# The last 32 tokens' expert rows by indirect DMA on VectorE, and the dense expert stage for 224 tokens

## The chip, the cores and the metric

One core of one Trainium2 chip runs the whole program. The metric is the device time of one execution in microseconds (us). The kernel before takes 1393.69 us, the median of 3 runs (1393.54 to 1394.06).

## The reference, cut to what matters

Two transformer blocks follow each other on 256 tokens of width 1024. The change touches only the last stage, the expert layer (PEER) of the second block. For each token, 8 heads choose 16 experts each out of 16384 (128 rows i by 128 columns j of a key grid), and each chosen expert e contributes gate * gelu(x . u_e) * v_e:

```python
def step(args):
    xc, ic, gc = args                 # tokens, chosen experts, gates
    u = expert_u[ic]
    hval = jnp.einsum('cd,chkd->chk', xc, u).astype(jnp.float32)
    a = (gc * jax.nn.gelu(hval, approximate=False)).astype(xc.dtype)
    return jnp.einsum('chk,chkd->cd', a, expert_v[ic])
```

The sum is added to the residual, and a last rms norm gives the output. All is float32.

## The kernel before, in words

The kernel gathers nothing. It computes the expert layer densely: U times x for all 16384 experts, the exact gelu, a dense matrix of gates that is zero for experts that were not chosen, the product of the two, and V times it. Experts go in 128 blocks of 128 (`NE`), in the order of the list `ORDER`.

Every weight of the program comes as a unit of 128 x 1024 float32 (512 KB). Four buffers each of `raw`, `wh` and `wl` hold it: SyncE issues the load, ScalarE rounds it to the high part (`high`, L1588, type fp32r), VectorE subtracts to get the low part (`low`, L567), and TensorE makes three fp32r products for each tile: high by high, high by low, low by high. So one unit costs ScalarE one pass of 1024 elements, VectorE one, and TensorE 6144 streamed columns. A buffer comes free when the step behind it is done, four units later. Each engine's order is the order of the code; there is no scheduler.

The expert layer has these stages.

- **U** (`early`, 128 units). The output is experts by tokens. Here the weights are the stationary operand and the 256 tokens are streamed. There are two forms. `unit_M` streams `hTb`, which holds the high and low parts of the tokens side by side, as 512 columns against the high weights, and 256 columns against the low weights: 16 matmuls. The second half of the bank must then be added to the first, by a copy on ScalarE (`block_out`) and a sum on VectorE (`summed`, or `both` early on). `unit_E` makes 24 matmuls of 256 columns, all into the same 256 columns, and needs neither. Units 0 to 31 and 48 to 127 take `unit_M`, units 32 to 47 `unit_E`. ScalarE then writes the gelu into `gates`.
- **Beside it**, during U units 0 to 47, VectorE does the two rounds of top-16 selection (`sixteen`, `at_rank` and what stands between, in slots of one `low` each). `best` tells that the choice is known.
- **G** (64 chunks of 4 tokens, one after each of U units 48 to 111). VectorE and ScalarE build one-hot rows (`oj`, `oi`), four plain float32 matmuls of 128 x 128 x 128 (eight instructions in the trace) multiply them out, and the chunk of gates is multiplied into what gelu has written, by `gated` and the lines behind it for what comes later.
- **V** (`unit_D`, 128 units). The output is tokens by 1024. Here the tokens' parts of `gates` are the stationary operand (two halves of 128 tokens, made by `high_of` and `low_of`), and the weights are streamed: 12 matmuls of 512 columns. The last four units are cut so that the tail can begin early.

GpSimd has nothing to do in all this. SyncE issues all DMAs. SBUF is filled to the end by `gates` (128 x 128 x 256 float32).

## Time and profile before

| | |
|---|---|
| median of 3 runs | 1393.69 us |
| span of the profiled execution | 1391.9 us |
| around the span (median less span) | 1.8 us |
| TensorE busy | 1379.2 us (99%) |
| VectorE busy | 1012.8 us (73%) |
| ScalarE busy | 850.9 us (61%) |
| GpSimd busy | 43.0 us (3%) |
| DMA, share of 16 engines in queue 1 | 53.1% |
| granted TensorE clock | 1.000 of 2.4 GHz |
| U stage begins, V stage begins | about 620 us, 1037 us |

A busy TensorE here means that a matmul is in flight; matmuls are pipelined and overlap, so the time of a piece of work is read from the distance between starts, not from the mean duration. The slices of the span show where an engine has room; the idle time in front of a group of instructions, and who ended it, tells what it waited for.

### The profile page before, as it was taken

Reading aid. Unit: us, or ns where it says so; the run is one execution under the profiler, and the core shown is the slowest. Engines: PE = TensorE matmul, PEld = TensorE weight load, DVE = VectorE, ACT = ScalarE, POOL = GpSimd, SP = SyncE. Lnnn points to the kernel's source line nnn. Section 1 sums busy time; section 2 is a strip of 40 time slices with the busy share of each in tenths; the row PEclk is TensorE's granted clock in tenths of the full one; section 3 lists DMA queues with packets and bytes.
Section 4 is the critical chain, followed back from the end, with each engine's and each line's share of the span. In section 5 each row is a group of like instructions: output and inputs, shape, how many; then the busy total and the mean of one; then the engine's idle time right before and its main releaser. Section 6 shows DMA issues by size and latency. Waiting matters only on the chain.

```text
span 1391.9 us, 20882 instructions
## 1 busy us (share of the span) xinstructions
PE 1379.2 (99%) x7704; PEld 1196.5 (86%) x7704; DVE 1012.8 (73%) x1926; ACT 850.9 (61%) x1647; POOL 43.0 (3%) x49
## 2 busy tenths in 40 slices
PE   8999999999999999999999999999999999999998
PEld 6998888888898888888899999999888888888886
DVE  6877776666786667689998888889776555555555
ACT  6875655555665554546767888888565455444554
POOL 3002030000000000000000000000000000000000
PEclk9999999999999999999999999999999999999999
DMA  6533466555444446545564444444466655566653
GB/s 228 183 113 129 143 216 190 188 182 182 165 158 146 137 152 226 188 161 165 184 202 158 142 151 137 149 139 144 160 213 222 214 193 192 192 195 195 194 191 101
DMA packets 67563, 240.85 MB, mean 173 GB/s; under 512 B 8453, under 2 KB 8965, under 8 KB 67078
## 3 DMA queue, kind: packets, MB, share of 16 engines
q1 hardware_dynamic: 67462, 239.52, 53.1%
q8 instruction: 62, 1.02, 0.3%
q14 instruction: 39, 0.32, 0.1%
HBM read 237.39 MB, written 2.10 MB: 172 GB/s over the span
## 4 chain that ended last, share of the span: by engine, by line
PE 94%; DVE 3%; ACT 2%; issue 1%; DMA 0%; POOL 0%; SPq 0%; POOLq 0%; ACTq 0%; DVEq 0%
PE bank L2239 92%; PE bank L2337 1%; PE bank L2325 1%; DVE wl L567 1%; ACT wh L1588 0%; DMA x<-in_x 0%; ACT kdz L1594 0%; DVE St L757 0%; DVE x L1066 0%; DVE sgt L1064 0%; DVE t L717 0%; DVE sg L711 0%; POOL st L487 0%; ACT h L1604 0%; DVE St L754 0%
## 5 line engine op out<-in xcount | busy, mean ns | idle before, releaser
L567 DVE TENSOR_TENSOR wl<-raw,wh 128x1024 fp32r<-128x1024 f32 x429 | 522.8, 1225 | 230.0 <-ACT wh L1588 229.0
L1588 ACT ACTIVATE wh<-raw 128x1024 fp32r<-128x1024 f32 x429 | 449.1, 1055 | 230.2 <-PE bank L2239 226.8
L2239 PE MATMUL bank<-hTb,wh 128*128 128x512 f32 (+2 forms) x1952 | 587.4, 363 | 0.0
L2239 PE MATMUL bank<-hTb,wl 128*128 128x256 f32 (+1 forms) x1640 | 432.7, 280 | 0.0
L2239 PE MATMUL bank<-wh,hTb 128*128 128x512 f32 (+1 forms) x1496 | 427.1, 392 | 0.9 <-DVE hTb L601 0.8
L2239 PEld LDWEIGHTS bank<-hTb,wh 128*128 128x128 f32 (+1 forms) x1952 | 341.2, 188 | 46.1 <-issue 0.3
L2239 PEld LDWEIGHTS bank<-wh,hTb 128*128 128x128 f32 x1496 | 281.1, 189 | 59.3 <-DVE wl L567 1.0
L2239 PEld LDWEIGHTS bank<-hTb,wl 128*128 128x128 f32 (+1 forms) x1640 | 309.5, 189 | 11.6
L2239 PE MATMUL bank<-wl,hTb 128*128 128x512 f32 (+1 forms) x748 | 245.9, 389 | 0.0
L2239 PEld LDWEIGHTS bank<-wl,hTb 128*128 128x128 f32 x748 | 141.2, 189 | 28.2
L2239 PEld LDWEIGHTS bank<-oi,oj 128*128 128x128 f32 x512 | 67.0, 191 | 2.9
L2239 PE MATMUL bank<-oi,oj 128*128 128x128 f32 x512 | 67.4, 274 | 0.0
L1594 ACT ACTIVATE us<-bank 128x256 f32<-128x256 f32 x80 | 30.2, 377 | 57.4 <-PE bank L2239 57.4
L1514 DVE TENSOR_TENSOR hTb<-gates,hTb 128x256 fp32r<-128x256 f32 x126 | 52.6, 418 | 0.0
L487 POOL TENSOR_TENSOR st<-st,mhalf 128x1 f32<-128x1 f32 (+2 forms) x15 | 13.1, 875 | 1269.9 <-DVE st L581 1000.2
L1594 ACT ACTIVATE hTb<-gates 128x256 fp32r<-128x256 f32 x126 | 50.3, 400 | 0.0
L1493 DVE TENSOR_TENSOR us<-bank,us 128x256 f32<-128x256 f32 x80 | 33.2, 415 | 17.4 <-ACT us L1594 17.4
L1475 DVE TENSOR_TENSOR oj<-iota,jT 128x512 f32<-128x512 f32 x64 | 43.6, 682 | 1.9 <-ACT gT L1594 1.9
L1487 DVE TENSOR_TENSOR gates<-gates,ga 128x256 f32<-128x256 f32 (+32 forms) x79 | 24.8, 314 | 25.2 <-ACT gates L2119 24.3
L2175 ACT ACTIVATE oi<-iota,iT 128x128 f32<-128x128 f32 x128 | 40.6, 391 | 0.0
L2179 ACT ACTIVATE oi<-oi,gT 128x128 f32<-128x128 f32 x128 | 40.6, 389 | 0.0
L1479 DVE TENSOR_SCALAR oi<-iota,iT,gT 128x128 f32<-128x128 f32 x128 | 35.5, 340 | 0.0
(396 smaller groups left out, 1264.2 us busy)
## 6 DMA issues: line engine op xcount, KB each, us to landing
raw<-in_wts SPq DMA_DIRECT2D x441, 512.0 KB, 4.2
x<-in_x SPq DMA_DIRECT2D x4, 256.0 KB, 5.2
sk<-in_sk SPq DMA_DIRECT2D x1, 1024.0 KB, 7.8
spill<-x SPq DMA_DIRECT2D x1, 1024.0 KB, 7.3
x<-spill SPq DMA_DIRECT2D x1, 1024.0 KB, 6.3
gb<-in_g_ffn SPq DMA_DIRECT2D x1, 512.0 KB, 4.8
gb<-in_norm_mix_g SPq DMA_DIRECT2D x1, 512.0 KB
gb<-in_norm_ffn_g SPq DMA_DIRECT2D x1, 512.0 KB, 5.7
```

What stands on the lines that cost most here:

```text
L567: e.tensor_tensor(b[:, :], raw[u % RAW][:, :], a[:, :].bitcast(F), ALU.subtract).then_inc(S("lo"), 1)
L1475: e.tensor_tensor(oj[c % NB][:, :, :], big, bc(jT[:, t], 2, 128), ALU.is_equal).then_inc(S("oj"), 1)
L1479: e.tensor_scalar(oi[c % NB][:, k, :], iota[:, :], iT[:, a], gT[:, a], ALU.is_equal, ALU.mult).then_inc(S("oi"), 1)
L1487: e.tensor_tensor(g[:, 0:c], g[:, 0:c], ga[n % 4][:, 0:c], ALU.mult).then_inc(S("gated_2"), 1)
L1493: e.tensor_tensor(u, B[2 + n % 4][:, 0:256], u, ALU.add).then_inc(S("u_sum"), 1)
L1514: e.tensor_tensor(b, gates[:, ORDER[n], :], a.bitcast(F), ALU.subtract).then_inc(S("al"), 1)
L1588: e.activation(parts_of(u)[0][:, :], raw[u % RAW][:, :], ACT.Copy).then_inc(S("hi"), 1)
L1594: return e.activation(o, i, ACT.Copy)
L2175: i = own.up(e.activation(oi[m][:, k, :], iota[:, :], ACT.Abs, scale=-1.0, bias=iT[:, t:t + 1]))
L2179: e.activation(oi[m][:, k, :], oi[m][:, k, :], ACT.Relu, scale=-2.0, bias=gT[:, t:t + 1]).then_inc(S("oi_act"), 1)
L2239: return e.matmul(o, l, r, start=first, stop=last, skip_group_check=True)
L2325: p = e.transpose(B[turned_at(t, i)[0]][:, two(128, k)], src[:, q, 512 * j + 128 * k:512 * j + 128 * k + 128], ident[:, :])
```

## The change

The expert layer is split by tokens. Tokens 0 to 223 (`TN`) stay in the dense form, with 224 in the place of 256 in U, gelu, gates and V, and 56 chunks of G (`NC`) for 64. Tokens 224 to 255 (partitions 96 to 127 of the second half) leave it: GpSimd copies their normalised rows, their experts' numbers and their gates to the layout 32 tokens by 4 groups of 32 choices, and then issues 64 indirect DMAs of 128 rows x 4 KB each, 32 from `u_rows` and 32 from `v_rows` (the same numbers in their plain layout in HBM), into three buffers. VectorE makes a dot product out of each of the first 32 (a fused multiply and sum), ScalarE one gelu, and VectorE multiplies each of the last 32 by its factor and adds it up. Three small DMAs bring the four groups together and VectorE adds them to the residual. These 64 slots stand in VectorE's order behind every second U unit from unit 104 (11 slots), and behind every second V unit (53 slots, up to V unit 106).

Besides, U units 0 to 31 and 48 to 103 change from `unit_M` to `unit_E`, all units below 104 being now 24 matmuls of 224 columns; units 104 to 127 (`SUMMED` on) stay `unit_M`, with 448 and 224 columns. In V the second half has 96 tokens; the streamed columns remain 512. The buffers for this come out of the smaller `gates`. Some semaphores are merged and their counts shifted.

```diff
 NP, NB = 47, 5
+TN = 224
+NC = TN // 4
+SUMMED = NP + 1 + NC
+SLOTS = 32
...
-        gates = M("gates", [128, 128, 256])
-        ga = [M(f"ga{i}", [128, 256]) for i in range(4)]
-        us = [sb("us0", [128, 256], F, X0 + 5120), M("us1", [128, 256])]
+        gates = M("gates", [128, 128, TN])
+        ga = [M(f"ga{i}", [128, TN]) for i in range(4)]
+        us = [sb("us0", [128, TN], F, X0 + 5120), M("us1", [128, TN])]
+        xr = sb("xr", [128, 1024], F, M.p)
+        acc = M("acc", [128, 1024])
+        ROWS = M.p
+        rows = [M(f"rows{i}", [128, 1024]) for i in range(3)]
+        fold = sb("fold", [128, 3, 1024], F, ROWS)
+        tq = sb("tq", [128, 2, 512], F, ROWS)
+        picked = sb("picked", [128, 128], U32, ROWS + 8192)
+        weight = sb("weight", [128, 128], F, ROWS + 8704)
+        expert = M("expert", [128, SLOTS], U32)
+        gate_of = M("gate_of", [128, SLOTS])
+        dots = M("dots", [128, SLOTS])
+        factor = M("factor", [128, SLOTS])
...
+        def used_by(j):
+            return j + 1 + 2 * (j >= SLOTS)
+        def slots_taken():
+            at = [n for n in range(SUMMED, NE - 2, 2)]
+            left = 2 * SLOTS - len(at)
+            return at, {2 * k + (2 if len(at) + k >= SLOTS else 0): len(at) + k for k in range(left)}
...
+            def four_ways(dst, src):
+                for a in range(4):
+                    e.dma_start(dst(a), src(a)).then_inc(S("in_few"), 16)
+            e.wait_ge(S("h"), 16)
+            four_ways(lambda a: xr[32 * a:32 * a + 32, :], lambda a: h5[96:128, 1, :])
+            e.wait_ge(S("in_few"), 64)
+            e.wait_ge(S("best"), 7)
+            four_ways(lambda a: expert[32 * a:32 * a + 32, :], lambda a: picked[96:128, two(SLOTS, a)])
+            four_ways(lambda a: gate_of[32 * a:32 * a + 32, :], lambda a: weight[96:128, two(SLOTS, a)])
+            e.wait_ge(S("in_few"), 192)
+            for j in range(2 * SLOTS):
+                if j >= 3:
+                    e.wait_ge(S("used"), used_by(j - 3))
+                k = j % SLOTS
+                e.indirect_dma_start(
+                    out=rows[j % 3][:, :], out_offset=None, in_=I["u_rows"] if j < SLOTS else I["v_rows"],
+                    in_offset=bass.IndirectOffsetOnAxis(ap=expert[:, k:k + 1], axis=0)).then_inc(S(f"in_rows{j % 3}"), 16)
+            e.wait_ge(S("used"), used_by(2 * SLOTS - 1))
+            for a in range(3):
+                e.dma_start(fold[96:128, a, :], acc[32 * a:32 * a + 32, :]).then_inc(S("in_few"), 16)
...
-                elif n < 16 + EARLY:
-                    n -= 16
-                    v = lows_of[:, n % 2, :]
-                    e.wait_ge(S("u_out"), nth_sum("U", n))
-                    e.tensor_tensor(v, B[2 + n % 4][:, 0:256], v, ALU.add).then_inc(S("u_sum"), 1)
...
+            few = slice(96, 128)
+            e.wait_ge(S("best"), 5)
+            e.wait_ge(own.sem, own.n)
+            e.scalar_tensor_tensor(out=picked[few, :].rearrange("p (h k) -> p h k", h=8), in0=ij[few, 0, 1, :, :],
+                                   scalar=128.0, in1=ij[few, 1, 1, :, :], op0=ALU.mult, op1=ALU.add).then_inc(S("best"), 1)
+            e.tensor_copy(weight[few, :].rearrange("p (h k) -> p h k", h=8), bst[few, 1, :, :]).then_inc(S("best"), 1)
...
+            def slot_taken(j):
+                t, k = rows[j % 3], j % SLOTS
+                e.wait_ge(S(f"in_rows{j % 3}"), 16 * (j // 3 + 1))
+                if j == 0:
+                    e.wait_ge(S("in_few"), 192)
+                if j < SLOTS:
+                    e.tensor_tensor_reduce(out=t[:, :], in0=t[:, :], in1=xr[:, :], scale=1.0, scalar=0.0, op0=ALU.mult,
+                                           op1=ALU.add, accum_out=dots[:, k:k + 1]).then_inc(S("used"), 1)
+                    return
+                if j == SLOTS:
+                    e.wait_ge(S("used"), used_by(SLOTS - 1) + 1)
+                    e.tensor_tensor(factor[:, :], factor[:, :], gate_of[:, :], ALU.mult).then_inc(S("used"), 1)
+                    e.wait_ge(S("used"), used_by(SLOTS - 1) + 2)
+                    e.tensor_scalar(acc[:, :], t[:, :], factor[:, 0:1], None, ALU.mult).then_inc(S("used"), 1)
+                    return
+                e.wait_ge(S("used"), used_by(j - 1))
+                e.scalar_tensor_tensor(out=acc[:, :], in0=t[:, :], scalar=factor[:, k:k + 1], in1=acc[:, :], op0=ALU.mult,
+                                       op1=ALU.add).then_inc(S("used"), 1)
+            def folded(a):
+                xs = x[few, 1, :]
+                if a == 0:
+                    e.wait_ge(S("in_end"), 48)
+                    e.wait_ge(S("used"), used_by(2 * SLOTS - 1))
+                    e.tensor_tensor(xs, xs, acc[few, :], ALU.add).then_inc(S("used"), 1)
+                    e.wait_ge(S("in_few"), 240)
+                e.wait_ge(S("used"), used_by(2 * SLOTS + a))
+                e.tensor_tensor(xs, xs, fold[few, a, :], ALU.add).then_inc(S("used"), 1)
...
-            for c in range(64):
+            for c in range(NC):
                 n = NP + 1 + c
-                summed(n)
                 low(nth("U", ORDER[n]) + 2)
-                if c + NB - 1 < 64:
+                if c + NB - 1 < NC:
                     one_hots(c + NB - 1)
                 gated(n)
...
+            at_u, at_v = slots_taken()
+            for n in range(SUMMED, NE - 2):
                 summed(n)
                 low(nth("U", ORDER[n]) + 2)
                 gated(n)
                 if n in (NE - 6, NE - 5):
                     low_of(n - NE + 6)
+                if n in at_u:
+                    slot_taken(at_u.index(n))
...
+                if n in at_v:
+                    slot_taken(at_v[n])
+                elif n - 6 in (max(at_v), max(at_v) + 1, max(at_v) + 2):
+                    folded(n - 6 - max(at_v))
...
-                if EARLY <= n <= NP:
+                if n < SUMMED:
                     e.wait_ge(S("done"), nth("U", ORDER[n]) + 1)
                 else:
                     e.wait_ge(S("u_sum"), nth_sum("U", n))
-                    b = lows_of[:, n % 2, :] if n < EARLY else us[n % 2]
+                    b = us[n % 2]
                 if c:
                     if n >= NP + 6:
                         e.wait_ge(S("gated_2"), n - NP - 5)
                     t = e.activation(ga[n % 4][:, 0:c], b[:, 0:c], ACT.Gelu)
-                if c < 256:
-                    t = e.activation(gates[:, ORDER[n], c:256], b[:, c:256], ACT.Gelu)
+                if c < TN:
+                    t = e.activation(gates[:, ORDER[n], c:TN], b[:, c:TN], ACT.Gelu)
                 t.then_inc(S("gelu"), 1)
             def block_out(n):
                 e.wait_ge(S("done"), nth("U", ORDER[n]) + 1)
-                if n < 2:
-                    e.wait_ge(S("u_sum"), nth_sum("w_peer_q_2", 14 + n))
-                elif n < EARLY:
-                    e.wait_ge(S("gelu"), n - 1)
-                copy(lows_of[:, n % 2, :] if n < EARLY else us[n % 2][:, :],
-                     B[2 + n % 4][:, 256:512]).then_inc(S("u_out"), 1)
+                copy(us[n % 2][:, :], B[2 + n % 4][:, TN:2 * TN]).then_inc(S("u_out"), 1)
...
-            for n in range(EARLY):
-                block_out(n)
-                if n:
-                    gelu(n - 1)
-                else:
-                    scores_out(3)
+            high(nth("U", ORDER[0]) + LOOK)
+            scores_out(3)
+            for n in range(39):
+                gelu(n)
...
+                if n == after_dots:
+                    e.wait_ge(S("used"), used_by(SLOTS - 1))
+                    e.activation(factor[:, :], dots[:, :], ACT.Gelu).then_inc(S("used"), 1)
...
-            def unit_E(unit, o, turned=None):
+            def unit_E(unit, o, turned=None, width=256):
                 wh_, wl_ = begin(unit)
                 for k in range(8):
                     c = two(128, k)
                     if turned is not None and k in (0, 4):
                         e.wait_ge(S("hT_lo"), 4 * turned + 3 + k // 4)
-                    mm(o, wh_[:, c], hTh[:, k, :], k == 0, False)
-                    mm(o, wh_[:, c], hTl[:, k, :], False, False)
-                    t = mm(o, wl_[:, c], hTh[:, k, :], False, k == 7)
+                    mm(o, wh_[:, c], hTh[:, k, 0:width], k == 0, False)
+                    mm(o, wh_[:, c], hTl[:, k, 0:width], False, False)
+                    t = mm(o, wl_[:, c], hTh[:, k, 0:width], False, k == 7)
...
-                        mm(bank[:, 0:256], wl_[:, c], hTh[:, k, :], False, False)
-                    t = mm(bank[:, :], wh_[:, c], hTb[:, :, k, :], k == 0, k == 7)
+                        mm(bank[:, 0:width], wl_[:, c], hTh[:, k, 0:width], False, False)
...
-            def part_D(held, xh, xl, base, q, first, last):
-                s = two(128, q)
+            def part_D(held, xh, xl, base, q, first, last, tokens=128):
+                s = slice(128 * q, 128 * q + tokens)
                 for a, b, f, z in ((xh, held[0], first, False), (xh, held[1], False, False), (xl, held[0], False, last)):
                     for n in range(2):
-                        t = mm(B[base + 2 * q + n][:, :], a[:, s], b[:, two(512, n)], f, z)
+                        t = mm(B[base + 2 * q + n][0:tokens, :], a[:, s], b[:, two(512, n)], f, z)
...
-                if n < EARLY or n > NP:
-                    unit_M(("U", ORDER[n]), B[2 + n % 4])
+                if n >= SUMMED:
+                    unit_M(("U", ORDER[n]), B[2 + n % 4], width=TN)
                 else:
-                    unit_E(("U", ORDER[n]), B[2 + n % 4][:, 0:256])
+                    unit_E(("U", ORDER[n]), B[2 + n % 4][:, 0:TN], width=TN)
...
-                unit_D(("D", "peer_expert_v_2", ORDER[n]), *of_expert(n), 0, n == 0, False)
+                unit_D(("D", "peer_expert_v_2", ORDER[n]), *of_expert(n), 0, n == 0, False,
+                       tokens=(rows_of(0), rows_of(1)))
...
-                        t = mm(end_of(c), a[:, 128:256], b[:, c], f, False)
+                        t = mm(end_of(c)[0:rows_of(1), :], a[:, 128:TN], b[:, c], f, False)```

TensorE in the stage with the gates: one U unit and the one-hot products behind it. Names are `hTb` for the tokens, `wh` and `wl` for high and low weights; the last number is the streamed width. Before:

```order
L2239 MATMUL bank<-oi_201,oj_196 128x128 x4
L2239 MATMUL bank<-hTb,wh_57 128x512
L2239 MATMUL bank<-hTb,wl_61 128x256
L2239 MATMUL bank<-hTb,wh_57 128x512
L2239 MATMUL bank<-hTb,wl_61 128x256
L2239 MATMUL bank<-hTb,wh_57 128x512
```

and the same place of the kernel after:

```order
L2332 MATMUL bank<-oi_201,oj_196 128x128 x4
L2332 MATMUL bank<-hTb,wh_57 128x224 x2
L2332 MATMUL bank<-hTb,wl_61 128x224
L2332 MATMUL bank<-hTb,wh_57 128x224 x2
L2332 MATMUL bank<-hTb,wl_61 128x224
L2332 MATMUL bank<-hTb,wh_57 128x224 x2
```

A pair of 512 and 256 columns has become a triple of 224 columns, eight times in a unit.

VectorE behind the last gate chunks, where U units go on without them (`us` is the sum of a bank's halves, `wl` the low part of a unit, `rows` and `dots` belong to the new slots). Before:

```order
L1493 TENSOR_TENSOR us_211<-bank,us_211 128x256
L567 TENSOR_TENSOR wl_62<-raw_54,wh_58 128x1024
L1487 TENSOR_TENSOR gates<-gates,ga_207 128x256
L1493 TENSOR_TENSOR us_212<-bank,us_212 128x256
L567 TENSOR_TENSOR wl_59<-raw_51,wh_55 128x1024
L1487 TENSOR_TENSOR gates<-gates,ga_208 128x256
```

and after:

```order
L1552 TENSOR_TENSOR us_211<-bank,us_211 128x224
L623 TENSOR_TENSOR wl_62<-raw_54,wh_58 128x1024
L1546 TENSOR_TENSOR gates<-gates,ga_207 128x224
L1561 ISA rows_215,dots<-rows_215,xr 128x1024
L1561 ISA dots 128x1
L1552 TENSOR_TENSOR us_212<-bank,us_212 128x224
L623 TENSOR_TENSOR wl_59<-raw_51,wh_55 128x1024
```

The dot product stands between one unit's product with the gates and the next unit's sum, and so ahead of the next unit's low part.

VectorE in the V stage, after (before, the rows L1561 are not there):

```order
L623 TENSOR_TENSOR wl_59<-raw_51,wh_55 128x1024
L1603 TENSOR_TENSOR hTb<-gates,hTb 128x224
L1561 ISA rows_217,dots<-rows_217,xr 128x1024
L1561 ISA dots 128x1
L623 TENSOR_TENSOR wl_60<-raw_52,wh_56 128x1024
L1603 TENSOR_TENSOR hTb<-gates,hTb 128x224
L623 TENSOR_TENSOR wl_61<-raw_53,wh_57 128x1024
```

One slot stands behind two units' low parts.

## Rows read from the trace of the kernel before

**Rows 1.** The page's busy line: busy us (share of the span) xinstructions.
```profile
PE 1379.2 (99%) x7704; PEld 1196.5 (86%) x7704; DVE 1012.8 (73%) x1926; ACT 850.9 (61%) x1647; POOL 43.0 (3%) x49
```

**Rows 2.** The chain of waits, end of it: start us, us, engine and line.
```profile
670.67 82.92 PE bank L2239 x584
754.25 620.40 PE bank L2239 x3304
1377.43 3.05 PE bank L2239 x12
```

**Rows 3.** Busy us (xinstructions) of each engine by stretch; clock, DMA share, GB/s.
```profile
660.00:711.00 51.00, 50.96 (x292) 44.23 (x291) 49.98 (x142) 34.74 (x58) 0.00 (x0) 1.00 0.56 186
711.00:757.00 46.00, 46.00 (x386) 46.00 (x386) 43.39 (x123) 31.54 (x52) 0.00 (x0) 1.00 0.62 205
800.00:900.00 100.00, 100.00 (x656) 90.70 (x656) 86.70 (x192) 84.33 (x247) 0.00 (x0) 1.00 0.46 143
992.00:1037.00 45.00, 45.00 (x259) 39.18 (x258) 32.34 (x51) 26.77 (x50) 0.00 (x0) 1.00 0.56 180
1087.00:1380.00 293.00, 292.92 (x1292) 242.28 (x1292) 167.32 (x215) 145.78 (x215) 0.00 (x0) 1.00 0.58 187
```

**Rows 4.** Timeline of TensorE, unit_M without gates: start us, us, instruction xcount.
```profile
1002.86 0.40 PE L2239 MATMUL bank<-hTb,wl 128*128 128x256 f32 x2
...
1011.31 0.40 PE L2239 MATMUL bank<-hTb,wl 128*128 128x256 f32 x2
1011.55 0.63 PE L2239 MATMUL bank<-hTb,wh 128*128 128x512 f32 x2
```

**Rows 5.** Timeline of TensorE, unit_E.
```profile
728.95 0.40 PE L2239 MATMUL bank<-hTb,wh 128*128 128x256 f32 x2
...
729.31 0.40 PE L2239 MATMUL bank<-hTb,wh 128*128 128x256 f32 x2
```

**Rows 6.** Timeline of TensorE, a gate chunk and a U unit in turn.
```profile
770.80 1.05 PE L2239 MATMUL bank<-oi,oj 128*128 128x128 f32 x8
771.61 0.48 PE L2239 MATMUL bank<-hTb,wh 128*128 128x512 f32 x1
...
774.47 1.05 PE L2239 MATMUL bank<-oi,oj 128*128 128x128 f32 x8
```

**Rows 7.** Timeline of TensorE, plain float32 products of 64 columns.
```profile
427.48 1.00 PE L2239 MATMUL bank<-v2b,PT 128*128 128x64 f32 x8
```

**Rows 8.** Timeline of TensorE, plain float32 products of 256 columns.
```profile
77.10 0.59 PE L2239 MATMUL bank<-kTn,qTn 128*128 128x256 f32 x2
77.53 0.59 PE L2239 MATMUL bank<-kTr,qTr 128*128 128x256 f32 x2
```

**Rows 9.** Timeline of TensorE, V stage; then a unit with 64 stationary columns.
```profile
1141.00 0.62 PE L2239 MATMUL bank<-wl,hTb 128*128 128x512 f32 x2
...
1142.36 0.62 PE L2239 MATMUL bank<-wl,hTb 128*128 128x512 f32 x2
...
25.16 0.39 PE L2239 MATMUL bank<-hTb,wh 128*64 128x256 f32 x2
...
25.50 0.39 PE L2239 MATMUL bank<-hTb,wh 128*64 128x256 f32 x2
```

**Rows 10.** VectorE, U units without gates: start us, us, instruction [idle before, releaser].
```profile
1009.59 0.42 DVE L1493 TENSOR_TENSOR us<-bank,us 128x256 f32<-128x256 f32 x1 [0.93 <-ACT us L1594]
1009.93 1.21 DVE L567 TENSOR_TENSOR wl<-raw,wh 128x1024 fp32r<-128x1024 f32 x1
```

**Rows 11.** VectorE groups by form: busy us, mean ns | idle us before, releaser.
```profile
L561 DVE SCALAR_TENSOR_TENSOR wl<-raw,gpc,wh 128x1024 fp32r<-128x1024 f32 x8 | 10.1, 1280 | 3.1 <-ACT wh L1585 3.1
...
L567 DVE TENSOR_TENSOR wl<-raw,wh 128x1024 fp32r<-128x1024 f32 x107 | 131.2, 1226 | 124.1 <-ACT wh L1588 124.1
```

**Rows 12.** DMA issues: KB each, median us to landing.
```profile
raw<-in_wts SPq DMA_DIRECT2D x103, 512.0 KB, 4.3
```

More of the change, by code:

```diff
@@ L1514, in low_of @@
                 e.tensor_tensor(b, gates[:, ORDER[n], :], a.bitcast(F), ALU.subtract).then_inc(S("al"), 1)
-            for n in range(NP + 65, NE - 2):
+            at_u, at_v = slots_taken()
+            for n in range(SUMMED, NE - 2):
                 summed(n)
@@ L1537, in add_end @@
                     c, b = two(512, 1), B[3][:, :]
-                e.tensor_tensor(x[:, 1, c], b, x[:, 1, c], ALU.add).then_inc(S("x"), 1)
+                xs = x[0:rows_of(1), 1, c]
+                e.tensor_tensor(xs, b[0:rows_of(1), :], xs, ALU.add).then_inc(S("x"), 1)
             def weighted_end(n):
                 c = ENDS[n]
+                e.wait_ge(S("used"), used_by(2 * SLOTS + 3))
                 e.wait_ge(S("x"), 19 + n)
@@ L2140, in keys_out @@
                 copy(key[a][:, s, :, :], bc(f4[:, s, a, :], 3, 16)).then_inc(S("key"), 1)
-            for n in range(EARLY):
-                block_out(n)
-                if n:
-                    gelu(n - 1)
-                else:
-                    scores_out(3)
+            high(nth("U", ORDER[0]) + LOOK)
+            scores_out(3)
+            for n in range(39):
+                gelu(n)
                 if n in (18, 19, 21, 23):
                     keys_out(0, n // 20, n % 18 in (1, 5))
-            high(nth("U", ORDER[EARLY]) + LOOK)
-            for n in range(EARLY - 1, 39):
-                gelu(n)
-                if 33 <= n < 37:
+                elif 33 <= n < 37:
                     keys_out(1, (n - 33) // 2, (n - 33) % 2)
@@ L2184, in scalar @@
             gelu(NP)
-            for c in range(64):
+            for c in range(NC):
                 n = NP + 1 + c
-                block_out(n)
-                if c + NB - 1 < 64:
+                if c + NB - 1 < NC:
                     one_hots(c + NB - 1)
@@ L2204, in high_of @@
                 copy(of_expert(n)[0], gates[:, ORDER[n], :]).then_inc(S("ah"), 1)
-            for n in range(NP + 65, NE - 2):
+            for n in range(SUMMED, NE - 2):
                 block_out(n)
@@ L2256, in unit_E, with unit_M @@
                         e.wait_ge(S("hT_lo"), 4 * turned + 3 + k // 4)
-                    mm(o, wh_[:, c], hTh[:, k, :], k == 0, False)
-                    mm(o, wh_[:, c], hTl[:, k, :], False, False)
-                    t = mm(o, wl_[:, c], hTh[:, k, :], False, k == 7)
+                    mm(o, wh_[:, c], hTh[:, k, 0:width], k == 0, False)
+                    mm(o, wh_[:, c], hTl[:, k, 0:width], False, False)
+                    t = mm(o, wl_[:, c], hTh[:, k, 0:width], False, k == 7)
                 t.then_inc(S("done"), 1)
-            def unit_M(unit, bank, turned=None):
+            def unit_M(unit, bank, turned=None, width=256):
                 wh_, wl_ = begin(unit)
@@ L2303, in unit_K, with unit_D @@
                 t.then_inc(S("done"), 1)
-            def part_D(held, xh, xl, base, q, first, last):
-                s = two(128, q)
+            def part_D(held, xh, xl, base, q, first, last, tokens=128):
+                s = slice(128 * q, 128 * q + tokens)
                 for a, b, f, z in ((xh, held[0], first, False), (xh, held[1], False, False), (xl, held[0], False, last)):
                     for n in range(2):
-                        t = mm(B[base + 2 * q + n][:, :], a[:, s], b[:, two(512, n)], f, z)
+                        t = mm(B[base + 2 * q + n][0:tokens, :], a[:, s], b[:, two(512, n)], f, z)
                 return t
-            def unit_D(unit, xh, xl, base, first, last, half=False):
+            def unit_D(unit, xh, xl, base, first, last, half=False, tokens=(128, 128)):
                 held = begin(unit)
                 for q in range(2):
-                    t = part_D(held, xh, xl, base, q, first, last)
+                    t = part_D(held, xh, xl, base, q, first, last, tokens[q])
                     if q == 0 and half:
@@ L2971, in tensor @@
             early(NP)
-            for c in range(64):
+            for c in range(NC):
                 early(NP + 1 + c)
@@ L2986, in tensor @@
                 p.then_inc(S("G_ps"), 1)
-            for n in range(NP + 65, NE):
+            for n in range(SUMMED, NE):
                 early(n)
```

66 lines of the change are left out of this document (37 added, 29 removed).

## The prediction

> **What bounds the kernel now.** I read the busy line first: TensorE is busy for 1379.2 of 1391.9 us, VectorE for 73%, ScalarE for 61% [rows 1]. The chain of waits agrees: its last links are TensorE alone, one of them 620.40 us long without a break, from 754.25 to 1374.65 [rows 2]. Next come the busy times by stretch. TensorE fills every stretch of the expert layer, its clock is the higher level throughout (1.00, so 2.4 GHz), and VectorE comes near to it in one place only, beside the first U units: 49.98 of 51 us and 43.39 of 46 us [rows 3]. So only a shorter TensorE stream can shorten the program, as long as VectorE, which now gets 64 large operations more, and the DMA engines still feed it in time. Since matmuls overlap, I price them by the distance between starts.
>
> **Prices on TensorE, from the rows.** A `unit_M` takes (1011.31 - 1002.86)/3 = 2.817 us, or 0.352 for a pair of 512 and 256 columns [rows 4]. A triple of 256 columns takes 729.31 - 728.95 = 0.36, so 0.120 each and 2.88 for a `unit_E` [rows 5]. A gate chunk and its U unit take 774.47 - 770.80 = 3.67, so the chunk costs 0.85 [rows 6]. In V six matmuls of 512 columns take 1.36, 0.2267 each and 2.72 a unit [rows 9]. From 256 to 512 columns the pitch grows by 0.1067, which is 0.417 ns a column, one column at each tick of 2.4 GHz; on top of the columns there are 13 ns.
>
> By columns alone, 224 would take 0.120 - 32 x 0.417 ns = 0.1067. But there is a floor under a narrow matmul: eight plain ones of 128 columns last 1.05, and eight of 64 columns last 1.00 [rows 6, 7]. Half the columns save 7 ns each and not 27 or more. Less the 0.28 that one of them lasts, the pitch is 0.77/7 = 0.110 for 128 and 0.103 for 64 columns. I take the load of 128 stationary columns to be what is left, and it is no smaller for fp32r of 224 columns. So I use 0.110 for 224 columns; the ends are 0.1067 (columns alone) and 0.120 (the narrower matmul brings nothing, since no row has an fp32r matmul below 256 columns).
>
> The Trainium skill, "TensorE: Matmul & The Clock Gate", section "Back-to-back issue gap", gives N/2.4 + 2.5 ns for the isolated warm matmul. That is 96 ns for 224 columns, and by it the time would be some 35 us below my forecast. The trace disagrees with it for this type: 256 columns take 120 ns [rows 5] where the rule has 109. The same page, section "LDWEIGHTS (loading the stationary operand)", has columns/1.2, so 107 ns for 128 of them, which would be the floor; as an estimate by this page the time would be about 8 us below mine. The sum below uses neither.
>
> **The change, part by part.**
>
> U stage, before: 112 `unit_M` x 2.817 = 315.5, 16 `unit_E` x 2.88 = 46.1, 64 chunks x 0.85 = 54.4; together 416.0. After: 104 `unit_E` of 224 columns at 24 x 0.110 = 2.64 make 274.6. 24 `unit_M` have pairs of 448 and 224 columns: 0.352 less 27 ns for the 64 columns less 7 to 10 ns for the other, 0.318, so 2.54 each and 61.1. 56 chunks make 47.6. Together 383.3: **32.7 us less**. With 0.1067 it is 42, with 0.120 only 6. The number of matmuls rises (24 for 16 in 88 units), which is why narrower streams do not bring the full eighth: in those units the change of form alone would cost 0.06 each.
>
> V stage: the 12 matmuls stream the weights, 512 columns each, for 96 tokens as for 128. Nothing goes by columns. The load of the stationary operand is shorter: with 64 stationary columns a triple of 256 takes 25.50 - 25.16 = 0.34 instead of 0.36 [rows 5, 9], 6.7 ns a matmul. Half of that for 96 columns, on 6 matmuls in 124 units, is **2.5 us less** (bounds 0 and 5).
>
> VectorE and ScalarE beside U units 0 to 103: the sums (0.42) and ScalarE's copies go. In the busiest stretch, where VectorE has 49.98 of 51 us [rows 3] at 2.82 a unit, it needs 0.42 less while TensorE needs 0.18 less, so it falls behind nowhere. In units 32 to 47, where no sum goes, its 43.39 us less one or two sums are at most 2.7 a unit against 2.64. That is even, and the lead of up to three units that it enters with covers the difference (bounds 0 and 1). With the gates it was busy for 86.7% [rows 3], 3.18 of 3.67; then 2.8 of 3.49. Cost 0. The two small operations that pack experts and gates are beside units that TensorE still has before it. Cost 0.
>
> The slots in the U stage: 11 of them. VectorE's own work is at hand: behind each TensorE unit it waits 0.93 for ScalarE's copy, then sum, then low part, which ends at 1009.93 + 1.21 = 1011.14, while TensorE needs it at 1011.55 + 0.23 = 1011.78 [rows 4, 10]. The lead is only 0.64, because `low` looks two units ahead here. The period shrinks by 0.28, narrower operations give back 0.05: lead 0.41, idle time 0.70. A fused multiply and sum is not in the trace; the nearest row is the 128x1024 operation with a scalar and two tensors, 1280 ns [rows 11], and I add 0.1 for the small instruction that follows it. 1.38 against 0.70 pushes the next sum, the low part behind it and the TensorE unit that waits for it: 0.68 - 0.41 = 0.27 each, **3 us more** for 11. If the fused one makes two passes (2.5), it is 1.4 each, 15 us; below, nothing.
>
> The slots in the V stage: 53, each behind two units. VectorE idles (1.226 busy, 124.1/107 = 1.16 idle before each low part [rows 11]) for 2.3 in two units, so 1.28 fits, and even 2.5 nearly does. `low` runs three units ahead here and waits for the release of a buffer, so nothing on TensorE waits. ScalarE's one gelu and the last additions fit into its 50% of idle time. Cost 0, and 4 at worst.
>
> The row transfers: 64 x 512 KB more. In V the DMA engines are at 0.58 for 187 GB/s [rows 3]. 53 transfers in 53 x 5.44 us are 96 GB/s on top, 283 in all, share 0.88 if it grows in step. A weight load lands in 4.3 us [rows 12]. It is issued when a low part ends, about 2.4 us behind the release of its buffer, and needed four units (10.9) behind that release, so it may take about 8.5. A row transfer is issued three slots ahead, 16 us. I take cost 0. No row shows an indirect transfer or any issued by GpSimd; the lower end is the weight load's 4.3, the upper one is open and is a rival below. The Trainium skill, "DMA: Bandwidth & Descriptors", section "Anatomy of one DMA — SWDGE (gpsimd) path", has 2.0 us + bytes/436 GB/s for GpSimd's DMAs, an estimate of 3.2 us here; no run here shows it.
>
> SyncE's queue keeps its order; GpSimd's one is empty at that time, and its last norm comes after the last row transfer, long before it is asked for.
>
> **Sum.** -32.7 - 2.5 + 3.0 = -32.2. The profiled span 1391.9 becomes 1359.7; the 1.8 us between span and median stay: **1361.5 us**.
>
> **Rivals.**
>
> (B) The narrow matmul brings nothing. fp32r at 224 columns keeps 0.117 to 0.120. For it: 13 ns stand on top of the columns at 256, and no row shows what they become below 256. Against: with 64 stationary columns 256 takes 0.113, so the stream itself is not the floor. The gain from U is 6 to 14, the time about 1385.
>
> (C) The slots can't be fed: row transfers or the fused operation are slow, VectorE stands in a slot, and the low parts behind it are late. For it: 32 more MB, a path unseen in the trace, one in-order VectorE that also feeds TensorE. Against: three buffers and 16 us. It decides from the point where a transfer takes more than one slot's 5.44 us in steady state; the gain is used up at 5.44 + 32.2/53 = 6.05. At 7 us it is 83 us more, about 1444; with a two-pass fused operation alone about 1374.
>
> (D) fp32r loses its single pass below some width, and all 224 columns streams with it. Plain float32 takes (77.53 - 77.10)/2 = 0.216 for 256 columns [rows 8], two ticks a column, where fp32r takes one. For it: every fp32r matmul of the trace streams at least 256 columns, so a limit there would never have shown. Against: nothing in the rows speaks for a limit. 224 columns would take 0.189, `unit_E` 4.54: 104 x 1.90 + 24 x 8 x 0.079 = 213 more, **1574 us**. If each plain float32 product's both instructions came back, some 2070. It decides from a pitch of 0.110 + 32.2/2496 = 0.123.
>
> **How the numbers follow.** Forecast 0.60, with its own range 1346 (columns alone, slots free, V's 5) to 1377 (two-pass dot). B 0.13, C 0.13, D 0.12, and 0.02 for what I do not see, a pitch of 0.096 (about 1326) among it. 8 times in 10 the time lies between 1346 and 1396: forecast, B and the mild part of C; D and the rest of C are left out. Within 0.2% (2.8 us, about what a measurement of this kernel can tell from no change) is 0.03, out of B and C. Faster has the forecast, most of B and a third of C, 0.76; slower 0.21.
>
> **What would show it.** In the profile after: a triple of 224 columns at 0.33 (0.32 columns alone, 0.36 is B, 0.57 or more is D); the U stage 383 us long; V units at 2.70 and no idle time of TensorE in V; waits of TensorE for the low part of 0.3 us at every second unit from 104 on; the fused operation at about 1.3. Rows L1561 with idle time ended by a DMA are C. I am wrong if the pitch of 224 columns leaves 0.107 to 0.120, or if TensorE waits in V at all.

## The result and the profile after

The kernel after takes **1372.34 us** (median of 4 runs, 1371.71 to 1373.34), the kernel before beside it 1393.62 (1393.48 to 1394.06): ratio **0.9847, interval 0.9833 to 0.9861**, faster by 21.3 us. The forecast was 1361.5 with a range of 1346 to 1396. The direction was right and the time lies in the range, but a third of the forecast gain is missing: 21.3 instead of 32.1 us.

The page's busy line after, which answers to [rows 1], with its DMA lines for GpSimd's queue and for the weights. PE is TensorE, PEld its weight loads, DVE VectorE, ACT ScalarE, POOL GpSimd.

```profile
PE 1357.3 (99%) x8344; PEld 1184.8 (86%) x8344; DVE 1045.3 (76%) x1909; ACT 804.7 (59%) x1512; POOL 159.7 (12%) x128
...
q0 software_dynamic: 9808, 34.51, 6.5%
...
raw<-in_wts SPq DMA_DIRECT2D x441, 512.0 KB, 3.5
```

TensorE remains the bound at 99%. The chain of waits shows where it is broken (start us, us, engine and line), against [rows 2]:

```profile
581.19 164.12 PE bank L2332 x1368
745.96 256.53 PE bank L2332 x2152
1002.56 350.11 PE bank L2332 x1536
```

The one link of 620 us has become two, and the gap between the last two rows, at 1002.5, is less than 0.1 us: 745.96 + 256.53 = 1002.49. So TensorE still works almost without a pause, and what is missing must be in how long its instructions take. The busy times by stretch, against [rows 3] (behind the comma PE, PEld, DVE, ACT, POOL, each with its instructions; then the clock, the DMA share and GB/s):

```profile
660.00:711.00 51.00, 51.00 (x459) 51.00 (x459) 47.78 (x141) 28.67 (x43) 0.00 (x0) 1.00 0.64 205
800.00:900.00 100.00, 100.00 (x898) 100.00 (x897) 81.48 (x169) 77.39 (x225) 0.00 (x0) 1.00 0.45 148
948.00:1010.00 62.00, 61.93 (x391) 57.84 (x390) 55.64 (x95) 38.09 (x73) 20.74 (x11) 1.00 0.76 280
1087.00:1350.00 263.00, 263.00 (x1145) 199.41 (x1144) 196.47 (x243) 127.47 (x192) 64.64 (x40) 1.00 0.76 264
```

Two readings. In the first two rows the weight loads (second column of busy times) now fill the stretch just as the matmuls do: 51.00 of 51 and 100.00 of 100, where before they had 44.23 and 90.70. That alone does not show that the loads set the pace: the `unit_E` with 256 columns of before had 46.00 of 46 too [rows 3], at a pitch of 0.120; e5 and e6 below test it. In the last row TensorE has no idle time, but runs 1145 matmuls; the kernel before, in a stretch of the same length inside its V stage, runs 1162:

```profile
1087.00:1350.00 263.00, 263.00 (x1162) 217.82 (x1162) 151.20 (x194) 131.81 (x194) 0.00 (x0) 1.00 0.60 194
```

That is 229.7 against 226.3 ns a matmul. TensorE's clock is the higher level (1.00) in all five rows.

By stages, from first matmul to first matmul:

| stretch | before | after | change | forecast |
|---|---|---|---|---|
| up to the first U unit | 618.0 | 617.4 | -0.6 | 0 |
| U stage with gates | 419.1 | 392.8 | -26.4 | -29.7 |
| V stage, 124 units | 337.3 | 342.3 | **+5.0** | **-2.5** |
| the rest | 17.5 | 17.5 | 0.0 | 0 |

### The profile page after: what moved, and what is told of

It is laid out like the page before. It is cut to its first block, busy times and chain, and to the rows that moved or that the text cites. A ratio compares the mean times of both kernels' runs of the same rounds, so it can differ in the third digit from the quotient of the medians.

```text
span 1370.0 us, 22081 instructions
## 1 busy us (share of the span) xinstructions
PE 1357.3 (99%) x8344; PEld 1184.8 (86%) x8344; DVE 1045.3 (76%) x1909; ACT 804.7 (59%) x1512; POOL 159.7 (12%) x128
## 3 DMA queue, kind: packets, MB, share of 16 engines
q0 software_dynamic: 9808, 34.51, 6.5%
## 4 chain that ended last, share of the span: by engine, by line
PE 93%; DVE 3%; ACT 2%; issue 1%; DMA 0%; POOL 0%; POOLq 0%; SPq 0%; ACTq 0%; DVEq 0%
PE bank L2332 91%; PE bank L2430 1%; DVE wl L623 1%; PE bank L2418 1%; ACT wh L1686 0%; ACT kdz L1692 0%; DVE St L813 0%; DMA x<-in_x 0%; DVE h L648 0%; DVE x L1122 0%; POOL st L519 0%; ACT h L1702 0%; DVE sgt L1120 0%; DVE t L773 0%; DVE sg L767 0%
## 5 line engine op out<-in xcount | busy, mean ns | idle before, releaser
L623 DVE TENSOR_TENSOR wl<-raw,wh 128x1024 fp32r<-128x1024 f32 x429 | 523.2, 1226 | 177.7 <-ACT wh L1686 174.4
L2332 PE MATMUL bank<-hTb,wh 128*128 128x224 f32 (+4 forms) x2656 | 566.4, 305 | 0.1
L2332 PEld LDWEIGHTS bank<-hTb,wh 128*128 128x128 f32 (+1 forms) x2656 | 424.1, 191 | 19.9 <-issue 1.3
L2332 PE MATMUL bank<-hTb,wl 128*128 128x224 f32 (+2 forms) x1640 | 439.7, 276 | 0.0
L2332 PE MATMUL bank<-wh,hTb 128*128 128x512 f32 (+1 forms) x1496 | 429.7, 394 | 1.3 <-DVE hTb L657 1.0
L2332 PEld LDWEIGHTS bank<-wh,hTb 128*128 128x128 f32 (+1 forms) x1496 | 267.1, 179 | 76.7 <-DVE wl L623 1.7
L2332 PEld LDWEIGHTS bank<-hTb,wl 128*128 128x128 f32 (+1 forms) x1640 | 312.5, 191 | 5.1
L2332 PE MATMUL bank<-wl,hTb 128*128 128x512 f32 (+1 forms) x748 | 247.0, 391 | 0.0
L2332 PEld LDWEIGHTS bank<-wl,hTb 128*128 128x128 f32 (+1 forms) x748 | 134.2, 179 | 36.2
L600 POOL DMA_INDIRECT rows<-in_u_rows,expert x32 | 54.4, 1699 | 306.5 <-DVE dots L1561 303.0
L600 POOL DMA_INDIRECT rows<-in_v_rows,expert x32 | 54.6, 1705 | 127.6 <-DVE acc L1571 107.3
L2332 PE MATMUL bank<-oi,oj 128*128 128x128 f32 x448 | 59.6, 276 | 0.0
L2332 PEld LDWEIGHTS bank<-oi,oj 128*128 128x128 f32 x448 | 54.5, 192 | 0.0
L1546 DVE TENSOR_TENSOR gates<-gates,ga 128x224 f32<-128x224 f32 (+28 forms) x79 | 24.2, 306 | 35.8 <-ACT gates L2217 34.9
L1603 DVE TENSOR_TENSOR hTb<-gates,hTb 128x224 fp32r<-128x224 f32 x126 | 48.4, 385 | 0.0
L1692 ACT ACTIVATE hTb<-gates 128x224 fp32r<-128x224 f32 x126 | 47.1, 375 | 0.0
L1571 DVE SCALAR_TENSOR_TENSOR acc<-rows,factor,acc 128x1024 f32<-128x1024 f32 x31 | 39.7, 1279 | 0.0
L1561 DVE CUSTOM_DVE_ANT_0 rows<-rows,xr 128x1024 f32<-128x1024 f32 x32 | 39.0, 1219 | 0.0
## 6 DMA issues: line engine op xcount, KB each, us to landing
raw<-in_wts SPq DMA_DIRECT2D x441, 512.0 KB, 3.5
gb<-in_g_ffn SPq DMA_DIRECT2D x1, 512.0 KB
gb<-in_norm_mix_g SPq DMA_DIRECT2D x1, 512.0 KB
gb<-in_norm_ffn_g SPq DMA_DIRECT2D x1, 512.0 KB, 4.5
```

The costliest lines, as they stand in the source:

```text
L600: e.indirect_dma_start(out=rows[j % 3][:, :], out_offset=None, in_=I["u_rows"] if j < SLOTS else I["v_rows"], in_offset=bass.IndirectOffse ...
L623: e.tensor_tensor(b[:, :], raw[u % RAW][:, :], a[:, :].bitcast(F), ALU.subtract).then_inc(S("lo"), 1)
L1546: e.tensor_tensor(g[:, 0:c], g[:, 0:c], ga[n % 4][:, 0:c], ALU.mult).then_inc(S("gated_2"), 1)
L1561: e.tensor_tensor_reduce(out=t[:, :], in0=t[:, :], in1=xr[:, :], scale=1.0, scalar=0.0, op0=ALU.mult, op1=ALU.add, accum_out=dots[:, k:k + ...
L1571: e.scalar_tensor_tensor(out=acc[:, :], in0=t[:, :], scalar=factor[:, k:k + 1], in1=acc[:, :], op0=ALU.mult, op1=ALU.add).then_inc(S("used ...
L1603: e.tensor_tensor(b, gates[:, ORDER[n], :], a.bitcast(F), ALU.subtract).then_inc(S("al"), 1)
```

## The experiments

e1 to e4 ran on one chip, where the kernel before had a median of 1393.54 (10 runs), e5 to e8 on another, where it had 1393.99 (9 runs). Two theories start from the table. **S**: a load of 96 stationary columns, which I had priced as a gain of 2.5 us, makes V slower. **P**: in U the load of 128 stationary columns sets the pitch of narrow matmuls, so a pair of 448 and 224 columns, of which only one is narrow, is cheaper than a triple of 224. The rivals of S are the row transfers and slots. Loading 96 columns and writing 96 rows of output are one and the same change here, so no run parts the two.

**e1, a whole stationary operand in V.** `whole(n)` is the full buffer in the place of its 224 columns.

```
-                unit_D(("D", "peer_expert_v_2", ORDER[n]), *of_expert(n), 0, n == 0, False,
-                       tokens=(rows_of(0), rows_of(1)))
+                unit_D(("D", "peer_expert_v_2", ORDER[n]), *(of_expert(n) if n < 2 else whole(n)), 0, n == 0, False,
+                       tokens=(128, 96 if n < 2 else 128))
...
```

> The kernel after, but V units 2 to 127 load 128 stationary columns in the second half again (columns 224 to 255 hold older values; the 32 rows that they make are never read). Theory S (the shorter load itself slows the 512-column matmuls: 2.76 us a V unit where it was 2.72): V units return to 2.72, 124 x 0.04 = 5 us faster than after, 1367. Rival T (traffic: row transfers and VectorE's slots read and write SBUF beside TensorE): V units stay at 2.76, 1372. My prediction's own term said that the shorter load gains 2.5 us; by it this kernel would be slower than after, 1375.

Measured: 1368.21 us (1367.1 to 1368.34), ratio 0.9815 (0.9802 to 0.9829), 4.1 below the kernel after. V takes 337.55 us. The timeline of TensorE in V, after and then e1 (start us, us, instruction):

```profile
1100.40 0.62 PE L2332 MATMUL bank<-wl,hTb 128*96 128x512 f32 x2
...
1101.78 0.63 PE L2332 MATMUL bank<-wl,hTb 128*128 128x512 f32 x2
...
1103.16 0.62 PE L2332 MATMUL bank<-wl,hTb 128*96 128x512 f32 x2
```

```profile
1199.81 0.62 PE L2332 MATMUL bank<-wl,hTb 128*128 128x512 f32 x2
...
1201.17 0.62 PE L2332 MATMUL bank<-wl,hTb 128*128 128x512 f32 x2
...
1202.53 0.62 PE L2332 MATMUL bank<-wl,hTb 128*128 128x512 f32 x2
```

Six matmuls take 1.38 us after and 1.36 in e1, the value of [rows 9]. Note that after, the halves with 128 and with 96 stationary columns both take 1.38: the slowdown is not confined to the matmuls that load 96. All slots and row transfers are still in e1, so they are not the cause. S holds.

**e2, no slots and no row transfers.**

```
-            for j in range(2 * SLOTS):
+            for j in range(0):
...
-                if n in at_u:
-                    slot_taken(at_u.index(n))
...
```

> The kernel after without the 64 indirect transfers, the 64 slots on VectorE, ScalarE's one gelu and the last additions (what the experts give to the last 32 tokens is left out). Theory S: V units stay at 2.76; only the waits of U units 104 to 127 go (61.7 us for 24 where 24 x 2.50 = 60.0), 1.7 us faster, about 1370.5. Rival T: V units return to 2.72 as well, 5 us more, about 1365.5. If the slots starved TensorE somewhere that I have not seen, more than that.

Measured: 1371.53 us (1370.78 to 1372.2), ratio 0.9841 (0.9826 to 0.9856), the same as the kernel after within what can be told. V's stretch in e2:

```profile
1087.00:1350.00 263.00, 263.00 (x1145) 199.44 (x1144) 145.85 (x192) 127.29 (x190) 0.00 (x0) 1.00 0.56 189
```

VectorE has 50 us less to do and the DMA engines 75 GB/s less to move, and TensorE still runs 1145 matmuls. In the U units from 104 on it is 1.3 us (60.40 for 61.67). So 64 large operations and 32 MB on a path that the trace of before did not have cost about one microsecond together in this kernel.

**e3, the kernel before with 96 columns in V's second half and nothing else.**

```
-                unit_D(("D", "peer_expert_v_2", ORDER[n]), *of_expert(n), 0, n == 0, False)
+                unit_D(("D", "peer_expert_v_2", ORDER[n]), *of_expert(n), 0, n == 0, False, tokens=(128, 96))
...
```

> The kernel before with 96 stationary columns in the second half of every V unit and nothing else of the change (32 tokens get nothing from the experts). Theory S: V units take 2.76 for 2.72, 5 us slower than before, 1398.7. Rival T: no difference, 1393.6. The prediction's term: 2.5 us faster, 1391.

Measured: 1398.82 us (1398.07 to 1399.39), ratio 1.0036 (1.0023 to 1.005): slower, by 5.3 us. TensorE's timeline in V:

```profile
1199.77 0.62 PE L2239 MATMUL bank<-wl,hTb 128*96 128x512 f32 x2
...
1201.15 0.63 PE L2239 MATMUL bank<-wl,hTb 128*128 128x512 f32 x2
...
1202.54 0.62 PE L2239 MATMUL bank<-wl,hTb 128*96 128x512 f32 x2
```

The same 1.385 as in the kernel after, out of a program that has only this part of the change. With e1 that is the effect from both sides: 4.1 us back when it is taken out, 5.3 us on top when it is put in (in V alone, by the traces, 4.8 and 5.0).

**e4, pairs beside the gates.** U units 48 to 103 go back to `unit_M` with 448 and 224 columns, with ScalarE's copy and VectorE's sum.

```
-SUMMED = NP + 1 + NC
+SUMMED = NP + 1
+TAIL = NP + 1 + NC
...
+                summed(n)
...
+                block_out(n)
...
```

> The kernel after with U units 48 to 103, those beside the gates, in pairs of 448 and 224 columns again, with ScalarE's copy and VectorE's sum. The trace after shows 0.3375 for a triple of 224 (2.70 a unit) and 0.312 for a pair of 448 and 224 (2.50 a unit). Theory P (TensorE sets the pace there, and the three products cost 0.2 a unit): 56 x 0.2 = 11 us faster than after, 1361. Rival Q (ScalarE, 3.08 us busy in a unit of the kernel before, or VectorE, 3.18, can't keep a pace of 3.37): waits of TensorE take half of it or more, 1367 to 1375.

Measured: 1363.93 us (1363.13 to 1365.03), ratio 0.9785 (0.9771 to 0.9798), 8.4 below the kernel after. The start of each gate chunk, after and then e4, and e4's busy times of that stretch:

```profile
751.15 1.06 PE L2332 MATMUL bank<-oi,oj 128*128 128x128 f32 x8
...
754.73 1.06 PE L2332 MATMUL bank<-oi,oj 128*128 128x128 f32 x8
```

```profile
802.03 1.05 PE L2335 MATMUL bank<-oi,oj 128*128 128x128 f32 x8
...
805.44 1.05 PE L2335 MATMUL bank<-oi,oj 128*128 128x128 f32 x8
```

```profile
800.00:900.00 100.00, 100.00 (x705) 96.50 (x705) 94.10 (x208) 88.23 (x263) 0.00 (x0) 1.00 0.47 156
```

The mean period of all chunks falls from 3.573 to 3.407, which is 9.3 us over 56. The expectation had 11 because it took 2.70 and 2.50 for units that take 2.68 and 2.52. VectorE rises from 81% to 94%. In the profiled run, the slowest of the five (1365.03), two pauses give part of it back: 1.8 us in the units from 104 on (63.51 for 61.67) and 0.8 in V (343.16 for 342.32). The first one (start us, us, instruction, idle time before it and what ended it):

```profile
990.21 1.06 ACT L1688 ACTIVATE wh<-raw 128x1024 fp32r<-128x1024 f32 x1 [1.91 <-DMA raw<-in_wts]
...
995.00 0.44 PE L2335 MATMUL bank<-hTb,wh 128*128 128x448 f32 x1 [1.89 <-DVE wl L624]
```

ScalarE waits for a weight load that lands late, the low part behind it is late too (a slot of VectorE stands between), and TensorE waits for it. In the kernel after ScalarE waits up to 2.16 us for a weight load at the start of V, and 2.08 at 1058, and TensorE never notices; without row transfers its longest such wait from 940 on is 1.41 (e2) and 1.81 (before), and both stand at the start of V. So P holds in its mechanism. That the row transfers make the loads late fits these rows, but was not tested in the kernel of e4.

**e5 and e6: what is the floor under a narrow matmul?** One run each. e5 streams 192 columns in the place of 224 in every `unit_E` of U, e6 loads 96 stationary columns in the place of 128.

```
-                    unit_E(("U", ORDER[n]), B[2 + n % 4][:, 0:TN], width=TN)
+                    unit_E(("U", ORDER[n]), B[2 + n % 4][:, 0:192], width=192)
```

> The kernel after with 192 instead of 224 streamed columns in the 104 U units of three products (tokens 192 to 223 get their hidden values from older contents of the bank, and so wrong expert sums). The trace after shows 0.1125 a matmul there. Theory F (a floor under the pitch that does not depend on the streamed columns): still 0.1125, the time stays at 1372. Rival C (the pitch goes by columns): 0.0992, 104 x 24 x 0.0133 = 33 us faster, 1339.

```
-                    unit_E(("U", ORDER[n]), B[2 + n % 4][:, 0:TN], width=TN)
+                    unit_E(("U", ORDER[n]), B[2 + n % 4][0:96, 0:TN], width=TN, experts=96)
...
```

> The kernel after with 96 instead of 128 stationary columns in the same 104 U units, 224 streamed (a quarter of the experts of these blocks is not computed). Theory L (the floor is the load of the stationary operand): the pitch falls to what the columns ask, 0.107 or, less 3 ns for the shorter load, 0.104: 104 x 24 x 0.006 to 0.009 = 15 to 21 us faster, about 1354. Rival I (the floor is a fixed cost of each matmul): still 0.1125, 1372. If shorter loads are as harmful as they are in the V stage, slower.

Measured: e5 1372.99 us, e6 1355.29 us. TensorE in a `unit_E`: after, e5, e6, in this order.

```profile
700.26 0.38 PE L2332 MATMUL bank<-hTb,wh 128*128 128x224 f32 x2
...
700.59 0.39 PE L2332 MATMUL bank<-hTb,wh 128*128 128x224 f32 x2
...
700.92 0.39 PE L2332 MATMUL bank<-hTb,wh 128*128 128x224 f32 x2
```

```profile
700.15 0.39 PE L2332 MATMUL bank<-hTb,wh 128*128 128x192 f32 x2
...
700.49 0.39 PE L2332 MATMUL bank<-hTb,wh 128*128 128x192 f32 x2
...
700.82 0.38 PE L2332 MATMUL bank<-hTb,wh 128*128 128x192 f32 x2
```

```profile
699.75 0.37 PE L2332 MATMUL bank<-hTb,wh 128*96 128x224 f32 x2
...
700.06 0.37 PE L2332 MATMUL bank<-hTb,wh 128*96 128x224 f32 x2
...
700.37 0.37 PE L2332 MATMUL bank<-hTb,wh 128*96 128x224 f32 x2
```

A triple takes 0.33 with 224 and 0.33 to 0.34 with 192 streamed columns: a seventh fewer columns bring nothing at all. With 96 stationary columns it takes 0.31. The groups of weight loads (busy us, mean ns of one), after and then e6, show the shorter load (the first also holds loads of other stages):

```profile
L2332 PEld LDWEIGHTS bank<-hTb,wh 128*128 128x128 f32 x2640 | 422.1, 191 | 19.8 <-issue 1.3 <-ACT pp L1692 0.2 <-DVE wl L623 0.2
```

```profile
L2332 PEld LDWEIGHTS bank<-hTb,wh 128*96 128x96 f32 x1664 | 221.3, 162 | 0.2 <-issue 0.2
```

So the pitch of these matmuls goes with the stationary columns, 0.112 with 128 of them and 0.104 with 96, and between 192 and 224 not with the streamed ones. That it is their load is the reading that fits; whether the load or the stream of 224 columns is the longer at 96, these runs don't tell. It matters which matmul a load lies beside: in a `unit_E` each one is beside a narrow matmul, while in a pair of 448 and 224 one of two is beside a wide one.

**e7, the kernel before with 96 stationary columns in both halves of V.** One run; is it the alternation of the two sizes that costs, or the 96 themselves?

```
-                unit_D(("D", "peer_expert_v_2", ORDER[n]), *of_expert(n), 0, n == 0, False)
+                unit_D(("D", "peer_expert_v_2", ORDER[n]), *of_expert(n), 0, n == 0, False, tokens=(96, 96))
...
```

> The kernel before with 96 stationary columns in both halves of V units 0 to 123 (64 tokens get nothing from the experts). Theory W (every load of 96 columns costs its matmul some ns): 2 x 5.3, about 1404. Theory A (the change of width between two loads costs it): V units return to 2.72 or less, 1393.6 or up to 5 us below.

Measured: 1398.17 us; V 342.24, as in e3 (342.26).

```profile
1200.06 0.62 PE L2239 MATMUL bank<-wl,hTb 128*96 128x512 f32 x2
...
1201.44 0.62 PE L2239 MATMUL bank<-wl,hTb 128*96 128x512 f32 x2
...
1202.82 0.62 PE L2239 MATMUL bank<-wl,hTb 128*96 128x512 f32 x2
```

1.38 again. Neither theory holds: alternation is not needed for the cost, and twice the number of short loads does not double it. The starts in e3's trace say how that comes about: from one matmul to the next it is 0.2300 between two with 96, as in e7, 0.2292 between two with 128, where the kernel before has 0.2267, and 0.231 to 0.233 at each change of size. What slows those with 128, and what the 3 ns a matmul are, stays open.

**e8, e1 and e4 together.** The edits are those two.

> The two gains together: pairs of 448 and 224 columns beside the gates, and 128 stationary columns in V. The V stage does not know of the U stage, so they add up: 1372.0 - 4.1 - 8.1 = 1359.8. If one takes from the other (VectorE enters V later), 1361 to 1364.

Measured: **1359.90 us** (1358.72 to 1361.78), ratio 0.9757 (0.9744 to 0.977). V takes 339.2 us, the gate period is 3.41, the units from 104 on take 61.69. It is the fastest of all the kernels here that compute everything, 12.4 us below the kernel after by medians. V's 339.2 are 1.7 above e1's 337.55; e8's row of the stretch 1087 to 1350 has 1163 matmuls in 262.95 busy us, so within it the pitch is e1's, and the difference lies outside it. It lies in three pauses at V's start, at 1006.8, 1012.6 and 1015.7, together 1.7 us:

```profile
1004.58 1.06 ACT L1688 ACTIVATE wh<-raw 128x1024 fp32r<-128x1024 f32 x1 [3.90 <-DMA raw<-in_wts]
...
1016.81 0.74 PE L2335 MATMUL bank<-wh,hTb 128*128 128x512 f32 x2 [0.72 <-DVE hTb L1605]
```

Again ScalarE waits for a late weight load, and VectorE, which has two slots between 1007 and 1016, is late with the tokens' low part that TensorE waits for. That the two gains add up to the expected 1359.8 is in part luck: e4's pause in the units from 104 on is gone, and this one has come.

## Why the prediction was right, and which terms were off

**The pitch of 224 columns: right in kind, 1.5% off in size.** The forecast took 0.110 from plain matmuls of 128 columns; 46 `unit_E` without gate chunks took 123.35 us, 2.68 each, pitch 0.1117. That is 4.2 us more over 104 units. The better value stood in the trace of before: but for the first of each eight, the plain matmuls of [rows 6, 7] start 0.110 to 0.112 apart, those of 64 columns as well as those of 128, while the prediction worked out 0.110 and 0.103 from the lengths of whole groups. Its reason, that the load of 128 stationary columns is what is left, was an inference in the prediction; e5 and e6 show that the floor goes with these columns. The Trainium skill, "TensorE: Matmul & The Clock Gate", "LDWEIGHTS (loading the stationary operand)", gives columns/1.2, that is 107 ns for 128 and 80 for 96. That is the time of a load, and the traces have pitches: 112 for 128 columns, near the rule, and 104 for 96, well above it, where the stream of 224 columns may be the longer of the two.

**The gate chunks: under-sized.** 55 periods from 751.15 to 947.68 make 3.573; less 2.68 that is 0.89 a chunk instead of 0.85, 2 us over all. The whole period is 32 times 0.1117, 24 matmuls of the unit and eight of the chunk at the same floor. The 0.85 came from a chunk between pairs of 512 and 256 columns. In e4, where the chunks stand between pairs of 448 and 224, 3.41 less 2.52 is 0.89 as well, so it is not the narrow matmul just ahead of the chunk that makes it dearer. Why it was cheaper beside 512 and 256 is open.

**U units 104 to 127 and their slots: 2.4 us better than forecast.** 61.7 us for 64.1. TensorE, and below it VectorE with a slot, after:

```profile
991.65 0.37 PE L2332 MATMUL bank<-hTb,wl 128*128 128x224 f32 x2
...
994.17 0.37 PE L2332 MATMUL bank<-hTb,wl 128*128 128x224 f32 x2
...
996.69 0.37 PE L2332 MATMUL bank<-hTb,wl 128*128 128x224 f32 x2
```

```profile
995.55 0.39 DVE L1552 TENSOR_TENSOR us<-bank,us 128x224 f32<-128x224 f32 x1
995.86 1.22 DVE L623 TENSOR_TENSOR wl<-raw,wh 128x1024 fp32r<-128x1024 f32 x1
...
997.70 0.39 DVE L1552 TENSOR_TENSOR us<-bank,us 128x224 f32<-128x224 f32 x1 [0.33 <-ACT us L1692]
```

A unit takes 2.52, a pair 0.315, where the forecast had 0.318. The slots cost 1.3 us in all (e2) and not 3: the sum behind a slot starts without idle time and the next one has waited 0.33 again, so VectorE has caught up within two units. TensorE's units take 2.51 to 2.63 there, and one 2.75; the waits of 0.3 us that the prediction named as a sign don't show. The fused operation takes one pass, as the forecast assumed:

```profile
L1571 DVE SCALAR_TENSOR_TENSOR acc<-rows,factor,acc 128x1024 f32<-128x1024 f32 x31 | 39.7, 1279 | 0.0
L1561 DVE CUSTOM_DVE_ANT_0 rows<-rows,xr 128x1024 f32<-128x1024 f32 x32 | 39.0, 1219 | 0.0
```

**The row transfers: right for this kernel.** The idle times before both operations are 0.0: VectorE never stood in a slot. GpSimd's issues and the wait ahead of them:

```profile
L600 POOL DMA_INDIRECT rows<-in_v_rows,expert x32 | 54.6, 1705 | 127.6 <-DVE acc L1571 107.3 <-DVE dots L1561 11.3 <-DVE acc L1568 8.9
L600 POOL DMA_INDIRECT rows<-in_u_rows,expert x32 | 54.4, 1699 | 306.5 <-DVE dots L1561 303.0
```

It is GpSimd that waits for VectorE to release a buffer, not the other way round. A transfer lands 5.9 us (median; 4.4 to 9.0) after its issue. That is longer than one slot, but they are issued up to three slots ahead, and the 9.0 stay under the 16 us. The term's weak side is the weight loads beside them, for which the prediction allowed 8.5 us: one takes 9.2 in this trace, and in e4 and e8 pauses of TensorE begin with a late one. The Trainium skill, "DMA: Bandwidth & Descriptors", "Anatomy of one DMA — SWDGE (gpsimd) path", led to an estimate of 3.2 us for each; the trace has nearly twice that, beside the weights' traffic, and the trace decides.

**The step that failed: "the load of the stationary operand is shorter ... 2.5 us less".** It cost 5.0 instead, 7.5 us of error and the largest single one. The price was carried over from matmuls of 256 columns with 64 stationary ones [rows 9] to matmuls of 512. With 256 columns the smaller operand came with a shorter pitch (0.113 for 0.120), with 512 columns a pitch of 0.2267 is twice the 0.112 of a load, and there was nothing to gain. The bounds, 0 and 5 us of gain, excluded a loss without a reason for that. e1 and e3 show that the 96 columns are the cause, e7 leaves the mechanism open.

Sum: +3.3 in the U stage, +7.5 in V and -0.6 ahead of U make 10.2, and 1359.7 + 10.2 = 1369.9, the profiled span of 1370.0 but for rounding. The range, 1346 to 1396, left room for an error of that size; the direction is right because the U stage brought 26.4 of its 29.7 us.

**The rivals.** B (the narrow matmul brings nothing, 1385) needed a pitch of 0.117 and more, and it is 0.112. C (slots not fed, 1374 to 1444) came within 2 us of the measured time with its two-pass form, but for a reason that the trace excludes: no wait of VectorE for a transfer, one pass of 1219 ns. A time near a rival's is no evidence for it. D (the single pass lost below some width, 1574) is refuted by 0.112, and by e5 down to 192 columns.
